# Differential attention's scores: half-array products in three steps against full-array products on doubled key and query parts

## What is computed

```
q = partial_rope(q.reshape(bsz, seq, 8, 2, 64), cos, sin) * (64 ** -0.5)
k = partial_rope(k.reshape(bsz, seq, 8, 2, 64), cos, sin)
...
s = einsum('nbhqd,nbhkd->nbhqk', q_blk, k)      # n: the two maps
p = softmax(s, axis=-1)
a = p[0] - lam * p[1]
o = einsum('bhqk,bhkd->bhqd', a, v)
```

## Time and profile before

| | |
|---|---|
| median of 3 runs | 3040.17 us |
| lowest, highest | 3035.26, 3040.46 us |
| span of the profiled execution (first to last instruction) | 3039.6 us |
| mean granted TensorE clock | 0.998 of full speed |
| PE busy | 2960.4 us, 97% |
| DVE busy | 1725.0 us, 57% |
| ACT busy | 1422.3 us, 47% |
| POOL busy | 421.7 us, 14% |
| queue of SP (hardware dynamic) | 42480 packets, 240.30 MB |
| other queues | instructions only |

### The profile page before, as it was taken

The page is one execution under the profiler, slowest core; times in us unless marked ns, Lnnn a source line. Parts: engine busy times, 40 slices in busy tenths (PEclk is TensorE's granted clock), DMA queues, the critical chain, the costliest instruction groups (busy, mean ns, idle before and its releaser), DMA issues. The chain is left out here.

```text
span 3039.6 us, 51611 instructions
## 1 busy us (share of the span) xinstructions
PE 2960.4 (97%) x20584; PEld 2383.2 (78%) x20584; DVE 1725.0 (57%) x2616; ACT 1422.3 (47%) x2795; POOL 421.7 (14%) x282
## 2 busy tenths in 40 slices
PE   9999989999999999999999999999999999999999
PEld 7788768777787878778777777778888877788887
DVE  7766742677437676733767445554444455554444
ACT  4555542666434555533666345763232356633322
POOL 1554510000013445400000020000000100000000
PEclk9999999999999999999999999999999999999999
DMA  4121112221222112112121222213222221122222
GB/s 151 64 83 59 51 59 89 73 75 60 84 88 98 64 64 85 42 66 91 60 74 60 106 87 87 77 49 111 97 97 97 84 87 62 51 98 98 95 97 83
DMA packets 42688, 243.17 MB, mean 80 GB/s; under 512 B 6832, under 2 KB 7792, under 8 KB 17136
## 3 DMA queue, kind: packets, MB, share of 16 engines
q1 hardware_dynamic: 42480, 240.30, 22.4%
HBM read 233.36 MB, written 2.20 MB: 77 GB/s over the span
## 5 line engine op out<-in xcount | busy, mean ns | idle before, releaser
L319 PE MATMUL bank<-hT,ws 128*128 128x512 f32 x2112 | 873.5, 414 | 12.7 <-issue 7.2
L323 PE MATMUL bank<-hT,ws 128*128 128x512 f32 x2112 | 827.5, 392 | 0.0
L322 PE MATMUL bank<-hT,ws 128*128 128x512 f32 x2112 | 825.9, 391 | 0.0
L319 PEld LDWEIGHTS bank<-hT,ws 128*128 128x128 f32 x2112 | 398.2, 189 | 96.9 <-issue 18.5
L276 DVE TENSOR_TENSOR ws<-raw,ws 128x2048 fp32r<-128x2048 f32 x160 | 372.7, 2330 | 164.7 <-ACT ws L270 161.6
L323 PEld LDWEIGHTS bank<-hT,ws 128*128 128x128 f32 x2112 | 397.3, 188 | 87.3
L270 ACT ACTIVATE ws<-raw 128x2048 fp32r<-128x2048 f32 x172 | 328.8, 1912 | 290.8 <-PE bank L319 175.5
L322 PEld LDWEIGHTS bank<-hT,ws 128*128 128x128 f32 x2112 | 399.0, 189 | 68.1 <-issue 1.4
L1113 PE MATMUL bank<-uS,ws 128*128 128x512 f32 x512 | 199.2, 389 | 0.0
L1116 PE MATMUL bank<-uS,ws 128*128 128x512 f32 x512 | 199.2, 389 | 0.0
L1117 PE MATMUL bank<-uS,ws 128*128 128x512 f32 x512 | 199.2, 389 | 0.0
(11 more groups left out here) (382 smaller groups left out, 4859.2 us busy)
## 6 DMA issues: line engine op xcount, KB each, us to landing
raw<-in_w_ff SPq DMA_DIRECT2D x64, 1024.0 KB, 4.7
raw<-in_w_delta SPq DMA_DIRECT2D x32, 1024.0 KB, 4.7
raw<-in_w_diff SPq DMA_DIRECT2D x32, 1024.0 KB, 4.7
raw<-in_w_att SPq DMA_DIRECT2D x20, 1024.0 KB, 4.8
raw<-in_w_merge_a SPq DMA_DIRECT2D x16, 1024.0 KB, 4.8
raw<-in_w_merge_b SPq DMA_DIRECT2D x16, 1024.0 KB, 4.8
raw<-in_w_out SPq DMA_DIRECT2D x16, 1024.0 KB, 4.8
rows<-sum_rows SPq DMA_DIRECT2D x16, 512.0 KB, 5.6
```

The costliest lines, as they stand in the source:

```text
L319: first = pe.matmul(out, hi, x[:, 0, k], start=(begin and k == steps[0]), stop=False)
L322: pe.matmul(out, hi, x[:, 1, k], start=False, stop=False)
L323: last = pe.matmul(out, lo, x[:, 0, k], start=False, stop=(end and k == steps[-1]))
```

## The change

Query and key are each brought, by four transfers, from `rq` into a buffer `both` of 128 partitions x 2 maps x 512, in which each map stands twice, in the lower and in the upper partitions. ACT rounds all of it, DVE makes the low part: for the query only in the upper partitions, so that `QS` is high over low; the key's high part `KH` and low part `KL` fill all 128. A map's scores are then two products of the full array: (query high over low) x (key high twice), and the same x (key low twice). This adds query low x key low, which was left out before. The orders on ACT, SP and PE are changed around it, the first weight split of head 1 moves from DVE to POOL, and a compiler setting for dynamic transfers is made smaller.

```diff
--- before.py
+++ after.py
@@ -2227,9 +2227,9 @@
      o_ready) = k.sems(
         "tile_ready", "tile_taken", "raw_ready", "q_rotated", "k_rotated", "qk_ready", "scratch_ready", "scratch_taken", "scores_ready",
         "max_ready", "exp_ready", "weights_ready", "weights_turned", "weights_t_ready", "o_ready")
-    osq, orms, on_ready, yt_ready, yhi, ylo, step, astep, cleared, qk_mixed, qk_high = k.sems(
+    osq, orms, on_ready, yt_ready, yhi, ylo, step, astep, cleared, qk_mixed, qk_high, *doubled = k.sems(
         "o_square", "o_rms", "o_normed", "y_t_ready", "y_high_done", "y_low_done", "diff_step", "diff_act_step",
-        "rotation_cleared", "qk_mixed", "qk_high_done")
+        "rotation_cleared", "qk_mixed", "qk_high_done", "query_doubled", "key_doubled")
     B, ps = k.bank, k.ps
     XB, SB, TB, OB = 2, 4, 6, (3, 7)
     HALF_ROPE = ROPE_DIM // 2
@@ -2244,7 +2244,11 @@
     with ExitStack() as ctx:
         room = Carve(k.cb[:, :], F32)
         rq, rot, zs = room(3, SEQ), room(2, SEQ), room(2, SEQ)
-        qk = k.sb(ctx, "qk", [P, 2, 2, 2, SEQ], F32R)
+        both = k.sb(ctx, "both", [P, 2, SEQ], F32)
+        QS = k.sb(ctx, "q_high_over_low", [P, 2, 2, SEQ], F32R)
+        KH = k.sb(ctx, "k_high_twice", [P, 2, 2, SEQ], F32R)
+        KL = k.sb(ctx, "k_low_twice", [P, 2, 2, SEQ], F32R)
+        UP = slice(64, P)
         vtm = k.sb(ctx, "vtm", [P, 2, NTOK, P], F32)
         pr = k.sb(ctx, "pr", [P, 2, 2, SEQ], F32)
         A = pr[:, :, 0]
@@ -2262,6 +2266,7 @@
             def _(pool):
                 k.clear_old(pool)
                 pool.memset(rot[:, :, :], 0.0).then_inc(cleared, 1)
+                st.low(pool, 1, 0)
 
             @block.sync
             def _(sp):
@@ -2271,11 +2276,20 @@
                     if h == 0:
                         sp.wait_ge(cleared, 1)
                     else:
-                        sp.wait_ge(qk_ready, nth(h - 1, 2, j))
+                        sp.wait_ge(qk_mixed, nth(h - 1, 2, j))
                     for m in range(2):
                         a, b = 64 * m, 64 * m + HALF_ROPE
                         sp.dma_start(rot[a:b, j], rq[b:b + HALF_ROPE, j]).then_inc(rotated[j], 16)
                         sp.dma_start(rot[b:b + HALF_ROPE, j], rq[a:b, j]).then_inc(rotated[j], 16)
+
+                def double(h, j):
+
+                    sp.wait_ge(qk_mixed, nth(h, 2, j))
+                    if 2 * h + j > 0:
+                        sp.wait_ge(qk_ready, 2 * h + j)
+                    for m in range(2):
+                        for to in range(2):
+                            sp.dma_start(both[64 * to:64 * to + 64, m], rq[64 * m:64 * m + 64, j]).then_inc(doubled[j], 16)
 
                 def refill(h, c):
                     st.taken(sp, h, c)
@@ -2287,11 +2301,15 @@
                 refill(0, 1)
                 swap(0, 0)
                 swap(0, 1)
+                double(0, 0)
+                double(0, 1)
                 refill(1, 0)
                 for h in range(1, HEADS):
                     swap(h, 0)
                     refill(h, 1)
+                    double(h, 0)
                     swap(h, 1)
+                    double(h, 1)
                     if h + 1 < HEADS:
                         refill(h + 1, 0)
                 following.load_after(sp, 0, 0)
@@ -2340,13 +2358,10 @@
                         pe.wait_ge(qk_ready, nth(h, 2, 1))
                     if u > 0:
                         pe.wait_ge(p_ready, 2 * u)
-                    for t, (a, b) in enumerate(((0, 0), (0, 1), (1, 0))):
-                        for m in range(2):
-                            hp = slice(64 * m, 64 * (m + 1))
-                            last = pe.matmul(B[SB + m][:, :], qk[hp, h % 2, 0, a, n * P:(n + 1) * P], qk[hp, h % 2, 1, b],
-                                             start=(t == 0), stop=(t == 2))
-                            if t == 2:
-                                last.then_inc(s_ready, 1)
+                    for m in range(2):
+                        q = QS[:, h % 2, m, n * P:(n + 1) * P]
+                        pe.matmul(B[SB + m][:, :], q, KH[:, h % 2, m], start=True, stop=False)
+                        pe.matmul(B[SB + m][:, :], q, KL[:, h % 2, m], start=False, stop=True).then_inc(s_ready, 1)
 
                 def turn_weights(u):
                     if u > 0:
@@ -2373,10 +2388,10 @@
 
                 fill = stream()
                 some(fill, 3 * KT + 4)
+                turn_v(0)
+                some(fill, 5)
                 scores(0)
-                some(fill, KT - 4)
-                turn_v(0)
-                some(fill, KT)
+                some(fill, KT - 1)
                 for u in range(UNITS1):
                     h, n = head(u)
                     if u + 1 < UNITS1:
@@ -2402,7 +2417,7 @@
                     act.wait_ge(tile, 4 * h + j + 1)
                     if h > 0:
                         if j < 2:
-                            act.wait_ge(qk_ready, nth(h - 1, 2, j))
+                            act.wait_ge(doubled[j], 64 * h)
                         else:
                             act.wait_ge(x_ready, scratch_use("v", h - 1) + 1)
                     act.activation(rq[:, j], B[j % 2][:, :], ACT.Copy, scale=0.125 if j == 0 else 1.0).then_inc(taken, 1)
@@ -2416,8 +2431,8 @@
                     act.activation(vtm[:, h % 2], B[XB][:, :].rearrange("p (c n) -> p c n", n=P), ACT.Copy).then_inc(x_taken, 1)
 
                 def qk_high_part(h, j):
-                    act.wait_ge(qk_mixed, nth(h, 2, j))
-                    act.activation(qk[:, h % 2, j, 0], rq[:, j], ACT.Copy).then_inc(qk_high, 1)
+                    act.wait_ge(doubled[j], 64 * (h + 1))
+                    act.activation((QS, KH)[j][:, h % 2], both[:, :, :], ACT.Copy).then_inc(qk_high, 1)
 
                 def z_gate(h):
                     act.wait_ge(tile, 4 * h + 4)
@@ -2449,25 +2464,27 @@
                 raw_copy(0, 0)
                 raw_copy(0, 1)
                 st.high(act, 1, 0)
+                qk_high_part(0, 0)
                 raw_copy(0, 2)
-                qk_high_part(0, 0)
                 qk_high_part(0, 1)
+                v_turned(0)
+                z_gate(0)
                 exps(0)
-                z_gate(0)
-                v_turned(0)
                 for u in range(UNITS1):
                     h, n = head(u)
                     more = h + 1 < HEADS
                     if n < 3 and more:
                         raw_copy(h + 1, n)
-                    if n in (1, 2) and more:
-                        qk_high_part(h + 1, n - 1)
+                    if n == 1 and more:
+                        qk_high_part(h + 1, 0)
                     if n == 0 and more:
                         st.high(act, h + 1, 1)
                     if u + 1 < UNITS1:
                         exps(u + 1)
                     act.wait_ge(at_turned, u + 1)
                     act.activation(AT[:, u % 2], B[TB][:, :], ACT.Copy).then_inc(at_ready, 1)
+                    if n == 2 and more:
+                        qk_high_part(h + 1, 1)
                     if n == 0 and not more:
                         following.second_high(act)
                     if n == 0 and h > 0:
@@ -2498,7 +2515,11 @@
 
                 def qk_low_part(h, j):
                     dve.wait_ge(qk_high, nth(h, 2, j))
-                    dve.tensor_tensor(qk[:, h % 2, j, 1], rq[:, j], qk[:, h % 2, j, 0].bitcast(F32), ALU.subtract).then_inc(qk_ready, 1)
+                    if j == 0:
+                        low = QS[UP, h % 2]
+                        dve.tensor_tensor(low, both[UP, :, :], low.bitcast(F32), ALU.subtract).then_inc(qk_ready, 1)
+                    else:
+                        dve.tensor_tensor(KL[:, h % 2], both[:, :, :], KH[:, h % 2].bitcast(F32), ALU.subtract).then_inc(qk_ready, 1)
 
                 def maxes(u):
                     for m in range(2):
@@ -2539,7 +2560,6 @@
                 mix(0, 1)
                 qk_low_part(0, 0)
                 qk_low_part(0, 1)
-                st.low(dve, 1, 0)
                 maxes(0)
                 weights(0)
                 for u in range(UNITS1):
@@ -3520,7 +3540,7 @@
     for n, g in zip(("gA", "gB"), gate_cols):
         arrays[n] = np.stack([np.ascontiguousarray(m.reshape(KT, P, -1).transpose(1, 0, 2)) for m in g])
     arrays.update(weight_chunks(x))
-    nc = _bacc.Bacc("TRN2", target_bir_lowering=False, num_devices=1)
+    nc = _bacc.Bacc("TRN2", target_bir_lowering=False, num_devices=1, dynamic_dma_scratch_size=2048)
     a = {n: nc.dram_tensor(f"in_{n}", v.shape, mybir.dt.from_np(v.dtype), kind="ExternalInput").ap() for n, v in arrays.items()}
     out = nc.dram_tensor("out_xT", (P, KT, SEQ), F32, kind="ExternalOutput").ap()
     build(nc, a, out)
```

## The result

| | before | changed |
|---|---|---|
| median of 5 runs | 3039.66 us | 3127.2 us |
| lowest, highest | 3035.26, 3040.46 us | 3122.7, 3128.24 us |
| span of the profiled execution | 3039.6 us | 3126.1 us |
| its mean granted TensorE clock | 0.998 | 0.992 |

The changed kernel takes 1.0292 times as long, 95% interval 1.0281 to 1.0303: 87.5 us more. The forecast was 3136 us, with a range of 3082 to 3165.

What follows compares the result with a forecast made beforehand. PE, busy 32.25 of 32.25 us in a head, was taken as the bound. A layer gains 4.5 + 5.1 + 6 x 5.5 - 0.2 = 42.4; 3039.6 + 85 for two layers + 11 for the clock gives 3136 us, range 3082 to 3165.

Steps and rivals of the forecast that it cites:

- the chain per head: From the query's mixed rows to the next head's first scores: 18.9 us, making them T+27.8 in head 0 instead of T+24.0.
- D: Wait from a mixed row to doubled copies, twice a head: 4.4 us, bounds 2.95 and 4.9; each us counts 32 us.
- The gain is 0.06 a unit: Score products on PE: four full-array products save 0.06 us a unit, 3.8 us over 64 units at most.
- The row-tile rule: Score products on PE: 64-row contractions let two row tiles run in parallel; by that half alone, full array adds 14.7 us.
- The start: Before the loop: both doublings in turn put first scores at 542.9 and the loop at 548.6, +4.5 us a layer.
- POOL's split: Weight split at the start moved to POOL: 7.4 us, ending at 536.1 before PE wants it at 538.8.
- I count half: Granted clock falling behind PE's 14 stops of 2.8 us: all would cost +22 us, half counted, +11.
- M: Time the query's rows are mixed, counted from T, a head's start: T+8.9, slipping to T+10.2 in heads after the first.
- Rival 1: New copies on SP's queue issued as briefly as loads: wait 2.95 us, 3079 us in all; between 3079 and 3105, chance 0.14.
- rival 2: Copies hidden before the key's low part is due at T+24, so PE gains: 3036 us, chance 0.04.
- rival 3: Full array is PE's slower form for the scores, nothing waiting: +14.7 us, 3054 us, chance 0.03.
- rival 4: Clock falls at every stop of PE and the copies' landing takes 2.2 us: 3165 us, chance 0.15.

Runs made afterwards that it cites:

- Experiment 2: Changed kernel without its 128 copies; the wider splits work on a buffer of zeros and wait for the mix alone: 3033.06 us, ratio 0.9978.
- experiment 6: Changed kernel with a second buffer, so the key's copies need not wait for the query's low part: 3102.98 us, ratio 1.0216.
- experiment 5: Changed kernel with the query's high part on ACT moved behind unit 1's exponentials, turned weights' copy and weight split: 3109.92 us, ratio 1.0235.
- experiments 3 and 4: Changed kernel with only the two copies crossing between halves: 3087.0 us; changed kernel with all four copies, each 8 of 64 partitions: 3120.12 us.
- experiment 1: Kernel before with only the score products changed, four full-array instead of six half-array ones, no copies: 3030.32 us, ratio 0.9969.
- experiment 11: Kernel before with only the weight split of head 1 at the start moved from DVE to POOL: 3046.59 us, ratio 1.003.

## Why the prediction was right, and where its sizes were off

**What bounds, and the chain per head: right.** PE had no slack, and the loss is the key's low part coming after PE is ready for it. Experiment 2 takes the copies out and the whole loss goes; experiment 6 takes out the one-buffer wait and 24 us go; experiment 5 takes ACT's wait ahead of the exponentials and PE's wait in unit 2 goes. The steps, forecast and measured:

| step | forecast | measured |
|---|---|---|
| high part, low part at 1,024 columns | 1.06, 1.22 | 1.06, 1.22 |
| D, from mixed rows to doubled | 4.4 | 4.2 |
| query's rows mixed, later heads | T+10.2 | T+9.95 |
| first scores of the next head | T+29.1 | T+28.2 |
| PE's stop there | 2.8 | 2.3 |
| PE's stop in unit 2 | 1.1 | 0.98 + 0.65 |
| period of a head | 37.8 | 37.0 |
| first scores of head 0 | 542.9 | 542.88 |

D was taken as the issues' 2.63 and a landing between two rows. The issues took 2.45, and experiments 3 and 4 show that it is their number that costs, not their bytes. Two of them are 1.2 us and 40 us of time, near the forecast's own slope, with the clock's part in it.

**"The gain is 0.06 a unit": mis-sized.** It is 0.13 to 0.14 a unit and 9.5 us in all by experiment 1, against 3.8. The step looked at the gap into the scores and up to the transposes, and not at the 0.06 that the transposes behind half-array products lose, which stood one row further in the same timeline. The row-tile rule of the Trainium skill, page TensorEngine Tiling (Array Packing), sections Key Properties and When to Use Tiling, would by its first half, two row tiles in parallel, have given a loss of 14.7 us. Experiment 1 shows a gain, so that half alone does not describe this unit. Its second half, the drain at a change of tiling mode, fits the gaps around the half-array products: 0.09 us in front of them, 0.20 more than three steps up to the transposes, and the 0.06 in the transposes. That the drain is their cause is not shown by itself.

**The start: order right, length short.** The first scores came where forecast, to 0.1 us, but by luck: SP began the copies at 528.94 instead of 529.32, D was 4.2 twice instead of 4.4, and 0.9 us that no step had made up for both. ACT's high part and DVE's low part of the query:

```profile
533.12 1.06 ACT L2435 ACTIVATE q_high_over_low<-both 128x1024 fp32r<-128x1024 f32 x1 [4.83 <-DMA both<-cb]
```

```profile
535.10 1.22 DVE L2520 TENSOR_TENSOR q_high_over_low<-both,q_high_over_low 64x1024 fp32r<-64x1024 f32 x1
```

The query's high part is done at 534.18 (533.12 and 1.06), but its low part, for which the key's copies wait, starts at 535.10, behind the key's mix, which POOL's split had stretched (experiment 11). In the second layer it is the same (1468.23 and 1469.16).

The loop came at 551.34 instead of 548.6. The difference is the clock, which the step on the start left out: PE had stood 4.03 us, and the products behind it are 0.43 apart instead of 0.23. Beside the forecast the loop is 3.1 us late in the first layer and 2.1 in the second, and the windows from 540 to 548 us put most of it down to the clock.

**"I count half" for the clock: near, by another sum.** 5 of 14 stops and both starts, against 7 of 14. Three whole heads with a fall behind the stop at their end last 38.08, 38.03 and 37.19 us, the second with four issues that took 3.28 instead of 2.45; those of heads 1 to 5 without one last 36.07 to 37.48. So about 1 us a fall is only an estimate. By it the falls at heads' stops are worth about 5 us, those at the starts up to 5, together near the 11 counted. The granted clock gives an upper bound: in windows of 1 us the nine falls took 18.7 us off full speed (3.4 each at the first start and behind the stop at 1512, 1.7 each of the others), part of it while PE stood anyway.

**POOL's split: forecast as free, and not quite.** It took 4.60 us, not 7.4. The trace of the kernel before holds twelve splits of this very size on POOL, in another phase, at 5.13 us (L276, 110.3 to 1235.6 us), a nearer row than the one scaled up. The step named PE's need and not what else POOL's work touches. It stretched an operation of DVE by 2.6. Of that 0.9 us in each layer reached the chain to the first scores, as shown above, and the rest passed while ACT waited for the query's copies; experiment 11 shows the price without that cover.

**The sum.** 85 and 11 were forecast, 87.5 came. The period was 0.8 too long (9.6 us over twelve heads: D's 0.2 twice, M's 0.25, small overlaps), the start 2.6 too short twice, PE's gain 5.7 too small, of which the unit's share in the period is part. The errors are small beside the sum because D, which carries 32 us for each us, was taken from the nearest rows: SBUF copies of the same kind at 0.62. Rival 1, short copies, is refuted by the issue row; rival 2 by the stop; rival 3 by experiment 1; rival 4, the clock at every stop, by 5 of 14. Rival 4's sum has a slip: landing at 2.2 instead of 1.75 makes D 0.45 longer, not 0.55, and its time 3 us less than 3165.

## What to carry to other kernels

Where an engine is busy all the time, cost a new transfer by the chain it is put into: count its issues on the queue one after another, add the landing, and look for the buffer that makes a second transfer wait for the first one's reader. The same arithmetic took 3127 and 3035 us; a second buffer, and an order in which no engine waits for a copy ahead of work that others need, made the difference. When an operation is moved past another, look up who waits for the one that it is moved past.

## What the runs showed of the hardware

- A DVE operation with both inputs in SBUF (128x512) that started while POOL ran its 128x2048 operation took 3.30 us instead of 0.69. In both kernels it ended 0.54 us behind POOL's (533.61 against 533.07, 534.61 against 534.07), so it hardly advanced until POOL was done. POOL's own lengths are rough in the profile. The Trainium skill, page SBUF — State Buffer, section SBUF: two separate sides, says that the two engines share a port pair that is locked for a whole instruction, and that a DVE operation with two SBUF inputs is one of those that need it, against a POOL operation that reads SBUF, as this one does. The trace agrees.
- Six half-array products in three steps and four full ones cost nearly the same on PE, and the full form wins by 0.08 before the transposes and 0.06 behind them.
- An SBUF-to-SBUF copy of 16 KB and one of 128 KB are issued in about the same time on SP's queue, 0.62 and 0.59 us (medians). Four in a row took about 2.45 in most heads of the changed kernel, but 2.9 to 3.3 in five of 28 (3.27 at 560.37, 3.28 at 1532.11); why is open.
- After stops of equal length (2.31 and 2.32 us) the granted clock once stayed at 1.00 and once fell. In experiment 5 it stayed behind one of 3.23 and fell behind one of 2.88, and in experiment 11 it stayed behind one of 2.79 and fell behind one of 2.80. What decides it stays open.
